# Half of each output projection multiplied between the heads of the attention, and added to x there

## Chip, cores and metric

One core of one Trainium2 chip runs the whole program. The metric is device microseconds (us) of one execution. Three timed executions of the kernel before took 4341.31 us in the median (4336.28 to 4342.41).

## The reference, cut to what matters

Two layers over 640 tokens (one tile of 128 context tokens, four tiles of 128 latent tokens), model width 1024. Each layer mixes tokens, adds the result to x, and then runs an expert network (PEER), which takes most of the time and is not touched here.

```
even layer:  oa = gated linear attention(h) -> rms_norm * silu      # (tokens, 512)
             ob = latent attention(h), 8 heads of 64                # (tokens, 512)
             x  = x + gate * (concat[oa, ob] @ w_out)               # w_out (1024, 1024)
odd layer:   oc = pool_mixer(h)                                     # (tokens, 512)
             od = windowed attention(h), 8 heads of 64              # (tokens, 512)
             x  = x + gate * (concat[oc, od] @ w_out)
```

The product with w_out is a sum over 1024 rows: 512 belong to oa (or oc), which is finished before the attention starts, and 512 to ob (or od).

## The kernel before, in words

Each engine has its own program (`block.tensor`, `block.vector`, `block.scalar`, `block.gpsimd`, `block.sync`), written out in order by hand; semaphores join them. Everything is float32.

**Streams of PSUM.** TensorE (PE) opens banks in order from three streams of two banks each: `open_d` (emptied by VectorE, DVE), `open_a` (emptied by ScalarE, ACT) and `open_s` (attention scores). `open_d` waits until all banks of its stream but the last one opened have been emptied (`d_free`). `copied()` waits until both streams are empty.

**The mixed vector.** `hT` holds eight slices of 128 rows: slices 0 to 3 are oa (or oc), written before the attention starts; slices 4 to 7 are the attention's output, written by `turn_out` (L645) once per tile.

**Attention.** `mla()` (even) and the second half of `odd()` loop over five query tiles `qt`. Tile 0 sees one key tile; tiles 1 to 4 of the even layer see five, of the odd layer three, four, four and three. `heads()` runs eight heads as a pipeline. Per turn of the loop PE does `scores(h + 2)` (L518), `turn(h + 1)`, the transposes of the softened scores (L532, L535), `product(h)` (L544), and then whatever `between(h)` holds. DVE does the maximum of the scores `biggest(h + 2)` (L1563; in the odd layer L1665, L1670), a reciprocal, the copy of the transposes `turned(h + 1)` (L1580), the scaling of the product (L1594), and then `between(h)`. ACT does the exponentials (L942, L973), in the even layer also the copy of the fifth transposed block (L846), and one square root per tile behind head 3, which needs a table load.

**Between the heads.** In both layers DVE prepares the next tile's queries there, in parts 0 to 5: part 3 (squares and their sum) behind head 3, part 4 behind head 4, part 5 (rotary embedding, L1479 to L1482) behind head 5. PE has queries work in the even layer alone, behind heads 0 to 2 (L599, L607). Tile 4 has no next tile and so nothing between its heads.

**Output projection.** `out_project` runs after the attention: two column halves `n` by five token tiles `t`, which is ten pieces. PE multiplies eight slices (L708); DVE multiplies the result by the gate (L1687) and adds it to x (L1689). Weights come through a ring of two slots, each 2 MB transfer issued by SyncE once the slot's last reader is done; `slot_done()` notes who that was. When the last sum is done, `x_done` lets the next norm start.

Of the kernel before, what the change touches and what calls it, by code (L numbers as in the profile page):

```python
# [26 lines left out]
ALU = mybir.AluOpType  # L27
# [52 lines left out]
def build_program(nc, a):  # L80

    ctx = ExitStack()
    with ctx:
# [208 lines left out]
        mod_rows = nc.dram_tensor("mod_rows", (2, 6 * D), F32, kind="Internal").ap()  # L292
        routing = nc.dram_tensor("routing", (NR, P, NB, RGROUP, TB), F32, kind="Internal").ap()

        def window_tiles(qt):

            return [0] if qt == 0 else [t for t in (qt - 1, qt, qt + 1) if 1 <= t < NT] + [5]
# [5 lines left out]
        def _(pe):  # L303
# [9 lines left out]
                pe.wait_ge(sem[f"slot_in{n % 2}"], 16 * (n // 2 + 1))  # L313
                return ring[:, n % 2, :]

            def slot_done():

                freed[item[0] - 1] = (last_stream[0], me.n[last_stream[0]])

            def mark(name):  # L320
                marks[name] = dict(me.n)
# [4 lines left out]
                pe.wait_ge(sem["a_free"], me.n["a_full"])  # L326

            last_stream = ["d_full"]

            def open_d():  # L330

# [189 lines left out]
            def heads(scores, probs_of, pT_of, tiles, v_of, between=None):  # L521
# [28 lines left out]
                for h in range(NH):  # L550
# [5 lines left out]
                    if between:  # L556
                        between(h)

            def mla():
                w = slot()  # L560
                w_uq = w[:, 0:2048].rearrange("p (k n) -> p k n", k=2)
                w_uk = w[:, 2048:3072].rearrange("p (k n) -> p k n", k=2)
                w_uv = w[:, 3072:4096].rearrange("p (k n) -> p k n", k=2)
                def keys_and_values(kt):
                    pe.wait_ge(*(me.due("ckv_ready") if kt < NT else (sem["ctx_in"], 32)))
                    ckv = pe_[:, kt, CKV0:CKV0 + 256] if kt < NT else ctx_ckv
                    out = open_d()
                    for k in range(2):
                        last = tr(out[:, P * k:P * (k + 1)], ckv[:, P * k:P * (k + 1)], ident)
                    last.then_inc(sem["d_full"], 1)  # L570
                    pe.wait_ge(sem["d_free"], me.n["d_full"])
                    for wk, opened, full in ((w_uk, open_d, "d_full"), (w_uv, open_a, "a_full")):
                        out = opened()
                        for k in range(2):
                            last = mm(out[:, :], ckvT[:, P * k:P * (k + 1)], wk[:, k, :], start=(k == 0), stop=(k == 1))
                        last.then_inc(sem[full], 1)

                keys_and_values(0)
                for kt in range(6):
                    if kt + 1 < 6:  # L580
                        keys_and_values(kt + 1)
                    pe.wait_ge(*me.due("k_ready"))
                    for g in range(2):
                        out = open_a()
                        for i in range(4):
                            h = 4 * g + i
                            last = tr(out[:, P * i:P * (i + 1)], qk[:, P * h:P * (h + 1)], ident)
                        last.then_inc(sem["a_full"], 1)
                    mark(("keys", kt))
                copied()  # L590
                turned_at = {}

                def queries(qt, part):

                    if part == 0:
                        pe.wait_ge(*me.due("ckv_ready"))
                        out = open_d()
                        for k in range(2):
                            last = tr(out[:, P * k:P * (k + 1)], pe_[:, qt, CQ0 + P * k:CQ0 + P * (k + 1)], ident)  # L599
                        last.then_inc(sem["d_full"], 1)  # L600
                        turned_at[qt] = me.n["d_full"]
                    elif part < 3:
                        at = 512 * (part - 1)
                        pe.wait_ge(sem["d_free"], turned_at[qt])
                        out = open_d()
                        for k in range(2):
                            last = mm(out[:, :], ckvT[:, P * k:P * (k + 1)], w_uq[:, k, at:at + 512],  # L607
                                      start=(k == 0), stop=(k == 1))
                        last.then_inc(sem["d_full"], 1)
                        if qt == NT - 1 and part == 2:  # L610
                            slot_done()

                for part in range(3):
                    queries(0, part)
                for qt in range(NT):
                    pe.wait_ge(*me.due("q_ready"))
                    for g in range(2):
                        out = open_a()
                        for i in range(4):
                            h = 4 * g + i  # L620
                            last = tr(out[:, P * i:P * (i + 1)], qk[:, P * h:P * (h + 1)], ident)
                        last.then_inc(sem["a_full"], 1)
                    copied()
                    tiles = [0] if qt == 0 else [1, 2, 3, 4, 5]
                    mark(("scores", qt))

                    def scores(h):
                        q_lhs = qT[:, P * h:P * (h + 1)]
                        if qt == 0:
                            attend(q_lhs, [(kT[:, h, 0:P], 0, P)])  # L630
                        else:
                            attend(q_lhs, [(kT[:, h, P:P + 512], 0, 512), (kT[:, h, P + 512:P + 640], 512, P)])

                    heads(scores, lambda h: probs[:, h % 2, :], lambda h: pT[:, h % 2, :], tiles,
                          lambda kt, h: vals[:, kt, 64 * h:64 * h + 64],
                          (lambda h: queries(qt + 1, h)) if qt + 1 < NT else None)
                    turn_out()

            def turn_out():
# [8 lines left out]
            def odd():  # L648
# [29 lines left out]
                for qt in range(NT):  # L678
# [8 lines left out]
                    def scores(h):  # L687
# [4 lines left out]
                        if qt:  # L692
# [2 lines left out]

                    heads(scores, lambda h: probs2[:, h % 2, :], lambda h: pT2[:, h % 2, :], tiles,
                          lambda kt, h: (po_[:, kt, VD0 + 64 * (h // 4):VD0 + 64 * (h // 4) + 64] if kt < NT
                                         else vctx[:, 64 * (h // 4):64 * (h // 4) + 64]))
                    turn_out()

            def out_project():
                copied()
                for n in range(2):
                    w = slot().rearrange("p (k n) -> p k n", k=KD)
                    for t in range(NT):
                        out = open_d()
                        for k in range(KD):
                            last = mm(out[:, :], hT[:, k, P * t:P * (t + 1)], w[:, k, :], start=(k == 0), stop=(k == KD - 1))  # L708
                        last.then_inc(sem["d_full"], 1)
                    slot_done()  # L710

            def route(l):
                copied()
# [575 lines left out]
        def _(dve):  # L1289
# [5 lines left out]
            def take_d():  # L1295
                n = me.next("d_full")
                dve.wait_ge(sem["d_full"], n)
                return bank[(n - 1) % 2]
# [200 lines left out]
            def mla():  # L1499
# [35 lines left out]
                def queries(qt, part):  # L1535
# [15 lines left out]
                    elif part == 5:  # L1551
                        if qt:
                            rope_into(qk3[:, :, 64:128], qk3[:, :, 64:128], qt, NH)
                        signal("q_ready")

                for part in range(6):
                    queries(0, part)
                for qt in range(NT):
                    n = P if qt == 0 else 5 * P

                    def biggest(h):
                        out = take_s().rearrange("p a b -> p (a b)")
                        link(V.tensor_reduce(stat[:, 32 + h:33 + h], out[:, 0:n], AX.X, ALU.max))  # L1563
                        give(ts(stat[:, 32 + h:33 + h], stat[:, 32 + h:33 + h], -MLA_SCALE, None, ALU.mult), "m_ready")

                    heads(biggest, lambda h: pT[:, h % 2, 0:min(n, 512)], att_o,
                          (lambda h: queries(qt + 1, h)) if qt + 1 < NT else None)

            def heads(biggest, pT_of, dst, between):

# [39 lines left out]
            def odd():  # L1610
# [36 lines left out]
                        signal("q_ready")  # L1647

                me.after("a_full", marks[("odd_k", 5)]["a_full"])
                for part in range(6):  # L1650
                    queries(0, part)
                for qt in range(NT):
# [8 lines left out]
                    def biggest(h):  # L1661
                        out = take_s().rearrange("p a b -> p (a b)")
                        s_ = soft_s[:, h % 2, :]
                        for i, (at, w, m_at) in enumerate(parts):
# [6 lines left out]
                        give(ts(stat[:, 32 + h:33 + h], stat[:, 32 + h:33 + h], sink[:, h:h + 1], -1.0,  # L1671
                                ALU.max, ALU.mult), "m_ready")

                    heads(biggest, lambda h: pT2[:, h % 2, 0:n], att_o2,
                          (lambda h: queries(qt + 1, h)) if qt + 1 < NT else None)

            def out_project(l):

                me.after("out_cache", 32 * (l + 1))
                if l:  # L1680
                    dve.wait_ge(sem["gates_in"], 16 * 4)
                for n in range(2):
                    for t in range(NT):
                        out = take_d()
                        g = gate[:, 0, int(t > 0), 512 * n:512 * n + 512]
                        tmp = arena[:, 8192:8704]
                        give(tt(tmp, out[:, :], g, ALU.mult), "d_free")  # L1687
                        xs = x[:, t, 512 * n:512 * n + 512]
                        ins = tt(xs, xs, tmp, ALU.add)  # L1689
                        if n == 0 or t < NT - 1:  # L1690
                            link(ins)
                give(ins, "x_done")
# [359 lines left out]
```

## Time and profile before

| what | us |
|---|---|
| median of three timed executions | 4341.31 |
| the profiled execution | 4340.67 |
| its span in the trace | 4338.9 |
| even layer, latent attention of tiles 1 to 4 | 565.5 to 725.4 |
| even layer, output projection | 725.4 to 795.9 |
| odd layer, windowed attention of tiles 1 to 4 | 2557.7 to 2715.4 |
| odd layer, output projection | 2715.4 to 2788.9 |

Times inside the trace are microseconds from the span's start. Busy shares say which engine is occupied in a stretch; the granted clock (PEclk) is the share of full speed at which TensorE was allowed to run, 1.00 for 2.4 GHz and 0.50 for 1.2 GHz. In a timeline the bracket behind a row is the engine's idle time before it and what ended that.

### The profile page before, as it was taken

To read this page: it belongs to the slowest core of one execution; us is meant where nothing else is said; L and a number is where in the kernel's file an instruction comes from. 1 tells how busy PE (TensorE), PEld (TensorE's weight loads), DVE (VectorE), ACT (ScalarE), POOL (GpSimd) and SP (SyncE) were. 2 spreads that over 40 slices of the span, in tenths; PEclk is the share of its full clock that TensorE was granted. 3 is DMA by queue.
4 is the path that set the end of the run, shared out by engine and by line. 5 is a ranking of instruction groups with operands and counts; after the bars stand their busy time and mean duration, and the time that the engine had idled before them with its cause. 6 is when DMAs were issued, how large, how long until landed. Compare 5 with 4: busy or idle time off the path is not lost. (4 is left out here: it accounts for less than half of the span.)

```text
span 4338.9 us, 51269 instructions
## 1 busy us (share of the span) xinstructions
PE 3786.7 (87%) x17467; PEld 2941.2 (68%) x17467; DVE 3316.4 (76%) x6040; ACT 1257.2 (29%) x1998; POOL 1940.3 (45%) x1290
## 2 busy tenths in 40 slices
PE   7986578899569999999997958886569999999997
PEld 1445255434458999999996547454458999999997
DVE  0116464487978999999998166299988999999998
ACT  1121122100553333333332132100563333333332
POOL 0000000001686777778775000000586777777775
PEclk9987689899789999999998955898799999999999
DMA  6210000242369999999998100111269999999997
GB/s 254 80 60 5 2 1 20 107 152 97 95 186 351 406 401 406 406 403 402 406 403 312 71 22 1 49 39 39 82 190 348 404 404 404 403 406 402 405 405 310
DMA packets 319360, 1013.07 MB, mean 233 GB/s; under 512 B 24062, under 2 KB 122366, under 8 KB 296728
## 3 DMA queue, kind: packets, MB, share of 16 engines
q0 software_dynamic: 152512, 571.76, 33.7%
q1 hardware_dynamic: 166744, 440.06, 26.9%
q8 instruction: 49, 0.80, 0.1%
q14 instruction: 55, 0.45, 0.0%
HBM read 958.16 MB, written 53.56 MB: 233 GB/s over the span
## 5 line engine op out<-in xcount | busy, mean ns | idle before, releaser
L1240 POOL DMA_INDIRECT arena<-in_peer_v,picked x512 | 831.9, 1625 | 226.7 <-issue 123.5
L1240 POOL DMA_INDIRECT arena<-in_peer_u_rows,picked x512 | 777.7, 1519 | 321.5 <-DVE dots L1817 194.1
L770 PE MATMUL pair<-h_hi,u_hi 128*128 128x384 f32 x2048 | 689.4, 337 | 30.9 <-issue 30.9
L770 PE MATMUL pair<-h_hi,u_lo 128*128 128x384 f32 x2048 | 688.8, 336 | 0.0
L770 PE MATMUL pair<-h_lo,u_hi 128*128 128x384 f32 x2048 | 688.0, 336 | 0.0
L1837 DVE SCALAR_TENSOR_TENSOR gate<-arena,act,gate 128x1024 f32<-128x1024 f32 x512 | 640.8, 1279 | 6.7 <-DVE act L1829 5.3
L1817 DVE CUSTOM_DVE_ANT_0 arena<-arena 128x1024 f32<-128x1024 f32 x512 | 612.4, 1219 | 17.1 <-DVE dots L1823 16.5
L1199 POOL TENSOR_TENSOR arena<-arena 128x256 f32<-128x256 f32 x192 | 287.3, 1530 | 348.9 <-DVE arena L1785 348.7
L770 PEld LDWEIGHTS pair<-h_hi,u_hi 128*128 128x128 f32 x2048 | 387.1, 189 | 39.2 <-issue 34.4
L770 PEld LDWEIGHTS pair<-h_lo,u_hi 128*128 128x128 f32 x2048 | 387.1, 189 | 4.8
L1029 ACT ACTIVATE u_hi<-ring 128x2048 fp32r<-128x2048 f32 x128 | 245.5, 1920 | 491.5 <-DMA ring<-in_peer_u 491.5
L770 PEld LDWEIGHTS pair<-h_hi,u_lo 128*128 128x128 f32 x2048 | 386.6, 189 | 0.0
L1049 ACT ACTIVATE act_raw<-pair 128x384 f32<-128x384 f32 x256 | 126.1, 492 | 809.6 <-PE pair L770 794.9
L1792 DVE TENSOR_TENSOR u_lo<-ring,u_hi 128x2048 fp32r<-128x2048 f32 x128 | 294.4, 2300 | 51.0 <-ACT u_hi L1029 46.2
L782 PE MATMUL bank<-v_hi,act_hi 128*128 128x512 f32 x1024 | 317.5, 391 | 0.0
L782 PE MATMUL bank<-v_hi,act_lo 128*128 128x512 f32 x1024 | 316.8, 391 | 0.0
L782 PE MATMUL bank<-v_lo,act_hi 128*128 128x512 f32 x1024 | 316.6, 390 | 0.0
L758 PE MATMUL pair<-arena 128*128 128x128 f32 x1536 | 223.9, 298 | 90.3 <-ACT arena L1012 49.7
L1785 DVE TENSOR_TENSOR arena<-arena,const 128x1024 f32<-128x1024 f32 x192 | 285.6, 1548 | 13.0 <-PE pair L758 9.8
L721 PE MATMUL bank<-hT,ring 128*128 128x128 f32 (+1 forms) x1024 | 292.8, 445 | 3.1 <-DVE hT L1362 3.1
L1796 DVE TENSOR_TENSOR v_lo<-ring,v_hi 128x2048 fp32r<-128x2048 f32 x128 | 292.6, 2286 | 0.0
L1279 POOL DMA_DIRECT2D arena<-in_subkeys x2 | 1.1, 542 | 641.7 <-DVE x L1689 641.7
(302 smaller groups left out, 5925.1 us busy)
## 6 DMA issues: line engine op xcount, KB each, us to landing
ring<-in_peer_u SPq DMA_DIRECT2D x128, 1024.0 KB
ring<-in_peer_v SPq DMA_DIRECT2D x128, 1024.0 KB
routing<-arena SPq DMA_DIRECT2D x24, 2048.0 KB, 8.7
arena<-routing SPq DMA_DIRECT2D x64, 768.0 KB
ring<-in_w_ada SPq DMA_DIRECT2D x12, 2048.0 KB, 7.7
ring<-in_w_ada POOLq DMA_DIRECT2D x12, 2048.0 KB, 8.0
ring<-in_peer_wq SPq DMA_DIRECT2D x8, 2048.0 KB, 7.8
ring<-in_w_in SPq DMA_DIRECT2D x6, 2048.0 KB, 7.8
```

The lines of the kernel that those rows point to most:

```text
L721: last = mm(out[:, 0:n], w[:, k, P * (g % 4):P * (g % 4 + 1)], hT[:, k, at:at + n], start=(k == 0), stop=(k == KD - 1))
L758: last = mm(pair[:, n % 4, P * q:P * (q + 1)], hots[:, n % 4, 1, q, :], hots[:, n % 4, 0, q, :], start=True, stop=True)
L770: last = mm(pair[:, j, 0:TD], R(u[b][:, P * (KD * j + k):P * (KD * j + k + 1)]), R(h[:, k, :]), start=(k == 0 and i == 0), stop=(k == KD - ...
L782: last = mm(outs_at[2 * t + half], R(w[b][:, j, P * t:P * (t + 1)]), R(v[b][:, D * j + 512 * half:D * j + 512 * half + 512]), start=False, ...
L1029: do(R(u_hi[b][:, :]), u_raw[b], ACT.Copy).then_inc(sem["u_led"], 1)
L1199: nc.gpsimd.tensor_tensor(rows, rows, bc(cols[:, b, 2, 4 * n + 2:4 * n + 4], P, 2), ALU.mult).then_inc(sem["gated_p"], 1)
L1240: pool.indirect_dma_start(gathered[:, b, :], None, rows, bass.IndirectOffsetOnAxis(picked[:, n:n + 1], 0)).then_inc(sem[f"row_in{b}"], 16)
L1785: tt(hots[:, m % 4], bc(cols[:, b, 0:2, 4 * n:4 * n + 4], P, 3), bc(bc(iota, 4, 1), 2, 1), ALU.is_equal).then_inc(sem["hot_ready"], 1)
L1792: tt(R(u_lo[b][:, :]), u_raw[b], u_hi[b][:, :], ALU.subtract).then_inc(sem["u_split"], 1)
L1796: tt(R(v_lo[b][:, :]), v_raw[b], v_hi[b][:, :], ALU.subtract).then_inc(sem["v_split"], 1)
L1817: V.tensor_tensor_reduce(gathered[:, b, :], gathered[:, b, :], h_nat[:, s_, :], 1.0, 0.0, ALU.mult, ALU.add, dots16[:, q:q + 1]).then_inc( ...
L1837: stt(acc[:, s_, :], gathered[:, b, :], act16[:, q:q + 1], acc[:, s_, :], ALU.mult, ALU.add).then_inc(sem["row_used"], 1)
```

## The change

Ten pieces per layer of the product with slices 0 to 3 are computed inside the attention's loop: `early_out((qt, h))`, called last in `between`. A table gives for each (qt, h) the piece (n, t). In the even layer the pieces stand behind heads (1, 3), (1, 6), (2, 3), (2, 6), (3, 3), (3, 7), (4, 1), (4, 3), (4, 5), (4, 7); in the odd layer behind heads 1, 4 and 7 of tiles 1, 2 and 3 and behind (4, 1). PE opens a bank of the d stream and multiplies four slices; DVE multiplies by the gate and adds to x, as before. `out_project` keeps ten pieces, but with slices 4 to 7 alone, and does the gate and the sum again for each. Both w_out weights now stay in the ring from the first early piece to the end.

```diff
+        early = [{(1, 3): (0, 0), (1, 6): (0, 1), (2, 3): (0, 2), (2, 6): (0, 3), (3, 3): (0, 4),
+                  (3, 7): (1, 0), (4, 1): (1, 1), (4, 3): (1, 2), (4, 5): (1, 3), (4, 7): (1, 4)},
+                 {(1 + i // 3, (1, 4, 7)[i % 3]): (i // NT, i % NT) for i in range(2 * NT)}]
...
 PE:
+            def early_out(at):
+                piece = early[layer[0]].get(at)
+                if piece is None:
+                    return
+                n, t = piece
+                if t == 0:
+                    w_out.append(slot().rearrange("p (k n) -> p k n", k=KD))
+                    out_items.append(item[0] - 1)
+                out = open_d()
+                for k in range(4):
+                    last = mm(out[:, :], hT[:, k, P * t:P * (t + 1)], w_out[-1][:, k, :], start=(k == 0), stop=(k == 3))
+                last.then_inc(sem["d_full"], 1)
...
 PE, out_project:
-                        for k in range(KD):
-                            last = mm(out[:, :], hT[:, k, P * t:P * (t + 1)], w[:, k, :], start=(k == 0), stop=(k == KD - 1))
+                        for k in range(4, KD):
+                            last = mm(out[:, :], hT[:, k, P * t:P * (t + 1)], w_out[n][:, k, :], start=(k == 4), stop=(k == KD - 1))
...
 DVE:
+            def add_out(n, t, tmp):
+                out = take_d()
+                link(tt(tmp, out[:, :], gate[:, 0, int(t > 0), 512 * n:512 * n + 512], ALU.mult))
+                signal("d_free")
+                xs = x[:, t, 512 * n:512 * n + 512]
+                return tt(xs, xs, tmp, ALU.add)
+            def early_out(at):
+                piece = early[layer[0]].get(at)
+                if piece:
+                    if layer[0] and piece == (0, 0):
+                        dve.wait_ge(sem["gates_in"], 16 * 4)
+                    link(add_out(*piece, pe_[:, 2, 0:512] if layer[0] == 0 else po_[:, 1, 0:512]))
```

## Rows read from the trace of the kernel before

**Rows 1.** The page: the span in 40 slices, granted clock in tenths.

```profile
PEclk9987689899789999999998955898799999999999
```

**Rows 2.** Windows: from:to, length; busy us (instructions) of PE, PEld, DVE, ACT, POOL; granted clock, DMA, GB/s.

```profile
653.40:697.70 44.30, 33.31 (x175) 25.30 (x175) 26.27 (x53) 13.87 (x30) 0.00 (x0) 0.88 0.13 48
697.70:725.40 27.70, 25.15 (x156) 19.71 (x156) 16.94 (x40) 9.90 (x25) 0.00 (x0) 0.94 0.01 2
725.40:795.90 70.50, 68.90 (x160) 30.32 (x160) 13.84 (x20) 0.00 (x0) 0.00 (x0) 1.00 0.10 33
2557.70:2595.20 37.50, 29.69 (x113) 24.90 (x112) 25.71 (x67) 12.38 (x30) 0.00 (x0) 0.50 0.00 1
2639.20:2683.00 43.80, 38.11 (x138) 30.46 (x140) 28.93 (x67) 12.84 (x29) 0.00 (x0) 0.50 0.00 1
2683.00:2715.40 32.40, 28.04 (x108) 23.51 (x107) 21.19 (x64) 8.62 (x25) 0.00 (x0) 0.50 0.00 1
2715.40:2721.60 6.20, 6.18 (x8) 2.59 (x9) 0.00 (x0) 0.00 (x0) 0.00 (x0) 0.50 0.01 3
2721.60:2788.90 67.30, 65.80 (x154) 28.85 (x152) 13.82 (x20) 0.00 (x0) 0.00 (x0) 1.00 0.10 35
```

**Rows 3.** Groups by line, even output projection: xcount, busy us, mean ns, idle before.

```profile
L708 PE MATMUL bank<-ring,hT 128*128 128x512 f32 x160 | 68.9, 593 | 0.8 <-issue 0.8
L1687 DVE TENSOR_TENSOR arena<-bank,gate 128x512 f32<-128x512 f32 x10 | 6.9, 692 | 57.8 <-PE bank L708 57.8
L1689 DVE TENSOR_TENSOR x<-x,arena 128x512 f32<-128x512 f32 x10 | 6.9, 692 | 0.3
```

**Rows 4.** Timeline (start, us, engine, line), even tile 3 around head 3.

```profile
672.28 0.33 SPq L1117 DMA_DIRECT2D ring<-in_w_out  x1
...
675.88 1.23 DVE L1544 TENSOR_TENSOR arena<-arena 128x1024 f32<-128x1024 f32 x1
...
676.41 0.27 PE L535 MATMUL bank<-const,ring 128*128 128x128 f32 x1
...
678.64 1.28 ACT L855 ACT_TABLE_LOAD   x1 [3.21 <-DVE stat L1316]
...
680.18 0.28 ACT L846 ACTIVATE arena<-bank 128x128 f32<-128x128 f32 x1
...
680.55 2.36 PE L544 MATMUL bank<-arena 128*128 128x64 f32 x10 [3.87 <-issue]
```

**Rows 5.** The page's DMA issues: the ring's 2 MB transfer, us from issue to landing.

```profile
ring<-in_w_in SPq DMA_DIRECT2D x6, 2048.0 KB, 7.8
```

**Rows 6.** Timeline, end of even tile 3 and start of tile 4.

```profile
692.22 1.30 PE L544 MATMUL bank<-arena 128*128 128x64 f32 x10 [2.08 <-DVE arena L1580]
...
693.97 1.05 PE L645 MATMUL bank<-const,arena 128*128 128x128 f32 x4 [0.45 <-DVE arena L1594]
694.82 2.07 PE L621 MATMUL bank<-const,arena 128*128 128x128 f32 x8
```

**Rows 7.** Windows of the even attention, columns as in rows 2.

```profile
649.60:653.30 3.70, 2.97 (x12) 2.27 (x12) 0.01 (x1) 1.77 (x3) 0.00 (x0) 0.54 0.00 0
653.30:656.70 3.40, 2.40 (x8) 1.28 (x8) 1.75 (x3) 0.77 (x3) 0.00 (x0) 1.00 0.00 0
...
680.40:687.20 6.80, 6.65 (x26) 5.64 (x26) 4.25 (x8) 2.50 (x5) 0.00 (x0) 0.50 0.00 0
```

**Rows 8.** Timeline, the scores of two successive heads, even tile 4.

```profile
705.74 1.35 PE L518 MATMUL pair<-ring,arena 128*128 128x512 f32 x4
...
708.54 1.35 PE L518 MATMUL pair<-ring,arena 128*128 128x512 f32 x4
```

**Rows 9.** Timeline, two successive heads of odd tile 3.

```profile
2654.30 2.07 PE L518 MATMUL pair<-arena 64*128 64x384 f32 x4
...
2656.49 0.69 DVE L1665 SCALAR_TENSOR_TENSOR arena<-pair,const 128x512 f32<-128x512 f32 x1 [1.55 <-PE pair L518]
...
2658.95 2.07 PE L518 MATMUL pair<-arena 64*128 64x384 f32 x4
```

More of the change, by code:

```diff
@@ L314, in slot, with slot_done @@
                 return ring[:, n % 2, :]
-            def slot_done():
-                freed[item[0] - 1] = (last_stream[0], me.n[last_stream[0]])
+            def slot_done(n=None):
+                freed[item[0] - 1 if n is None else n] = (last_stream[0], me.n[last_stream[0]])
             def mark(name):
@@ L328, in _ @@
             last_stream = ["d_full"]
+            w_out, out_items = [], []
             def open_d():
@@ L557, in heads @@
                         between(h)
+            def early_out(at):
[10 more added lines that the diff above has]
+                last.then_inc(sem["d_full"], 1)
             def mla():
                 w = slot()
+                w_item = item[0] - 1
                 w_uq = w[:, 0:2048].rearrange("p (k n) -> p k n", k=2)
@@ L610, in queries @@
                         if qt == NT - 1 and part == 2:
-                            slot_done()
+                            slot_done(w_item)
                 for part in range(3):
@@ L632, in scores, with between @@
                             attend(q_lhs, [(kT[:, h, P:P + 512], 0, 512), (kT[:, h, P + 512:P + 640], 512, P)])
+                    def between(h):
+                        if qt + 1 < NT:
+                            queries(qt + 1, h)
+                        early_out((qt, h))
                     heads(scores, lambda h: probs[:, h % 2, :], lambda h: pT[:, h % 2, :], tiles,
-                          lambda kt, h: vals[:, kt, 64 * h:64 * h + 64],
-                          (lambda h: queries(qt + 1, h)) if qt + 1 < NT else None)
+                          lambda kt, h: vals[:, kt, 64 * h:64 * h + 64], between)
                     turn_out()
@@ L697, in odd @@
                           lambda kt, h: (po_[:, kt, VD0 + 64 * (h // 4):VD0 + 64 * (h // 4) + 64] if kt < NT
-                                         else vctx[:, 64 * (h // 4):64 * (h // 4) + 64]))
+                                         else vctx[:, 64 * (h // 4):64 * (h // 4) + 64]),
+                          lambda h: early_out((qt, h)))
                     turn_out()
@@ L703, in out_project @@
                 for n in range(2):
-                    w = slot().rearrange("p (k n) -> p k n", k=KD)
                     for t in range(NT):
                         out = open_d()
-                        for k in range(KD):
-                            last = mm(out[:, :], hT[:, k, P * t:P * (t + 1)], w[:, k, :], start=(k == 0), stop=(k == KD - 1))
+                        for k in range(4, KD):
+                            last = mm(out[:, :], hT[:, k, P * t:P * (t + 1)], w_out[n][:, k, :], start=(k == 4), stop=(k == KD - 1))
                         last.then_inc(sem["d_full"], 1)
-                    slot_done()
+                    slot_done(out_items[n])
+                w_out.clear()
+                out_items.clear()
             def route(l):
@@ L1554, in queries, with between @@
                         signal("q_ready")
+                def between(qt, h):
+                    if qt + 1 < NT:
+                        queries(qt + 1, h)
+                    early_out((qt, h))
                 for part in range(6):
@@ L1566, in mla @@
                     heads(biggest, lambda h: pT[:, h % 2, 0:min(n, 512)], att_o,
-                          (lambda h: queries(qt + 1, h)) if qt + 1 < NT else None)
+                          lambda h: between(qt, h))
             def heads(biggest, pT_of, dst, between):
@@ L1649, in odd, with between @@
                 me.after("a_full", marks[("odd_k", 5)]["a_full"])
+                def between(qt, h):
+                    if qt + 1 < NT:
+                        queries(qt + 1, h)
+                    early_out((qt, h))
                 for part in range(6):
@@ L1672, in biggest @@
                                 ALU.max, ALU.mult), "m_ready")
-                    heads(biggest, lambda h: pT2[:, h % 2, 0:n], att_o2,
-                          (lambda h: queries(qt + 1, h)) if qt + 1 < NT else None)
+                    heads(biggest, lambda h: pT2[:, h % 2, 0:n], att_o2, lambda h: between(qt, h))
+            def add_out(n, t, tmp):
[10 more added lines that the diff above has]
+                    link(add_out(*piece, pe_[:, 2, 0:512] if layer[0] == 0 else po_[:, 1, 0:512]))
             def out_project(l):
                 me.after("out_cache", 32 * (l + 1))
-                if l:
-                    dve.wait_ge(sem["gates_in"], 16 * 4)
                 for n in range(2):
                     for t in range(NT):
[L1684 to L1689, printed above, removed]
+                        ins = add_out(n, t, arena[:, 8192:8704])
                         if n == 0 or t < NT - 1:
```

## The prediction, made before the change was run

> **What bounds the kernel now.** I read the clock line of the page first, then windows by stage, then the timeline inside one tile of each layer. The expert stages fill most of the span at full clock and are not touched; the change concerns two stretches of about 230 us each. In the clock line [rows 1] the attention stages show as the dips to 8 (even) and to 5 (odd), so every matmul moved into them has to be priced at the clock granted there.
>
> The windows [rows 2] show three situations. In both output projections PE is busy 66 to 69 of 67 to 70 us at clock 1.00 and DVE 14: PE alone sets their end, and each of the ten pieces takes 68.9 / 10 = 6.89 us for eight slices, so 3.44 us for four [rows 3]. DVE needs 0.69 + 0.69 = 1.38 us per piece, hidden under the next piece. In the even attention PE is busy 33.3 of 44.3 us in tile 3 (tiles 1 and 2 look alike) at a mean clock of 0.88: it waits for other engines. In tile 4, which prepares no next queries, it is busy 25.2 of 27.7. In the odd attention the clock is 0.50 from end to end, PE is busy 38.1 of 43.8 us in tile 3 and DVE 28.9.
>
> The profiled execution took 4340.67 us, of which 1.8 lie outside its span; it is 0.6 below the median of the timed runs, so its sums carry over.
>
> **Even layer.** Removed: half of every piece of the projection, 10 x 3.44 = -34.4 us. DVE's 1.38 us per piece is still shorter than the 3.44 us that are left, so PE still sets the end.
>
> Pieces (1,3), (2,3), (3,3). After head 3's transposes PE stands idle for 3.87 us [rows 4]: the copy of the fifth transposed block is behind ACT's square root and its table load, and that waits for DVE's queries part 3. In the new order PE has the piece exactly there: the bank it needs is free before part 3 begins, so 3.44 us fit into 3.87. DVE takes up the piece after part 3 and spends 1.38 us before its next maximum; but the exponential that follows waits for the second table load anyway, so that delay mostly disappears. PE now has no gap, while before it ran the next 6.8 us at half clock [rows 7]. I take -0.5 each, -1.5 together (bounds: +1.4, DVE's part uncovered, and -2, if the clock gives back more).
>
> Pieces (1,6), (2,6), (3,7). At the tile's tail PE waits for DVE, which is in the rotary embedding, and the last product comes 2.08 us late [rows 6]. A piece behind head 6 needs a bank that only DVE's copy of head 7 frees, the same copy that the product waits for. So it starts no earlier than that product did and pushes it by 3.44. Behind head 7 it adds 3.44 plus 0.69 for the multiply, because `turn_out` waits until both streams are empty. But PE stays busy where it had idled, and the next transposes, 2.07 us for eight [rows 6], and the next tile's first scores would run at full clock: about 1.7 us back. So +2 each, +6 (bounds +1 to +5 each).
>
> Pieces (4,1), (4,3), (4,5), (4,7). A head of tile 4 takes 708.54 - 705.74 = 2.80 us [rows 8] with PE working back to back, nothing to hide in: 3 x 3.44 = 10.3, and 3.44 + 0.69 = 4.1 for (4,7), in front of the last `turn_out`. +14.4 (bounds 13 and 17). DVE idles while PE does the piece and then owes 1.38 us, PE's next scores take 1.35 of it [rows 8], and the exponential is not due for three steps.
>
> The second w_out block is issued at 672.28 [rows 4] and such a block lands after 7.8 us [rows 5], ahead of piece (3,7) near 693. It is released by the last queries matmul as before. The peer_wq blocks wait, as before, for the two halves of the projection; one comes 17 us before the end, enough for 7.8. SP and POOL issue the same transfers in the same order. Sum of the even layer: -34.4 - 1.5 + 6 + 14.4 = -15.5 us.
>
> **Odd layer.** Removed: -34.4 again. The first 6.2 us of this projection ran at 0.50 [rows 2]; it will still start from low clock, so this part is neither gained nor lost.
>
> Added: ten pieces. At half clock a piece is 6.9 us, at full clock 3.44. Nothing in the trace of before runs such matmuls between odd heads, so the bounds are 69 and 34 us for ten. What the clock does in front of a rise: in the projection it rose 6.2 us after dense matmuls began [rows 2], in the even layer after a stretch of 2.97 us busy [rows 7]. Heads of the odd layer keep PE busy before a piece already, which is why I take a value near the shorter: 3.3 us at low clock, which does half of that, 1.65 us' worth, and the remaining 1.8 at full clock. That is 5.1 us per piece.
>
> Given back: after the rise PE runs the following heads fast for a while. A head of tile 3 takes 4.65 us, in which DVE waits 1.55 for the scores [rows 9]; that wait goes, in the heads with no queries part. Behind head 7 the next tile's start gains, 2.1 us of scores per head at half clock [rows 9]. I count 1.7 us back per piece; DVE's 1.38 us of a piece is inside the first fast scores or costs up to 0.8, counted in this. So 5.1 - 1.7 = 3.4 per piece, +34 for ten. Each second piece stands behind head 4, where DVE has part 4 of the queries to do meanwhile; the bank rule makes PE wait there for the copy of head 5, which cancels that. Sum of the odd layer: -34.4 + 34 = about 0.
>
> The transfer of the gates for this layer is long over when the first piece asks for it, since it is issued when x of layer 0 is done, near 2376, 180 us earlier.
>
> Total: -15.5 + 0, so 4340.7 - 15.5 = 4325 for the profiled execution and 4326 against the median.
>
> On the clock the Trainium skill ("TensorE: Matmul & The Clock Gate", Part 4: PE-mode transpose) says that the full clock does not engage for transposes because they don't count as PE-busy in the same way. This trace disagrees: between 649.6 and 653.3 PE ran nothing but twelve transposes, and the clock then rose from about half to 1.00 [rows 7]. If the rule held it would be the fourth rival below.
>
> **Rivals.**
> 1. The odd heads stay at full clock once a piece has raised it. Then DVE bounds a tile: 28.9 us of work, 3 x 1.38, about 7 of start and tail, 40 instead of 43.8 for tiles 2 and 3; likewise 37 for 37.5 and 29 for 32.4 [rows 2], together 12 us less than before with the pieces inside. With -34.4 and 3 more from the projection's start: -49, in all -65, 4277. For it: the even heads mostly keep full clock. Against it: PE was busy 38 of 43.8 us at half clock and the clock never rose [rows 2]; at full clock the same work would leave PE idle for about half of the time.
> 2. The clock does not rise between odd heads, or falls at once: a piece costs 6.9 us behind PE that is already busy without a pause. +69 - 34.4 = +34 there, in all +19, 4360. It decides from 5 us net per odd piece, (34.4 + 15.5) / 10. Against it: the projection does start a rise within less than one old piece.
> 3. Pure displacement: the work is moved and nothing is hidden. Even pieces cost 3.44 each plus the multiplies, odd pieces 3.4 to 4: +-8, 4339. For it: eight of ten odd slots and four even ones lie where PE never waits.
> 4. Transposes keep no clock. Then nothing is given back after a piece: even tails cost 3 x 1.7 more, odd pieces 5.1 each. +5 and +17: +7, 4348. Against it the row just named. This is what the page of the Trainium skill cited above would make of it.
>
> **How the numbers follow.** My forecast 0.50 (its own range 4313 to 4335), rival 1 0.12 (also in part, 4280 to 4313), rival 2 0.12, rival 3 0.21, rival 4 0.05. A measurement of this kernel can tell about 0.2%, 8.7 us, from no change. Below 4332.6 lie most of the forecast (0.43) and all of rival 1: 0.55. Within 0.2% the rest of the forecast, rival 3 and half of rival 4: 0.32. Above 4350: rival 2 and some of rival 4: 0.13. The range for 8 in 10, 4300 to 4347, leaves out most of rival 1 and rival 2.
>
> **What would show it.** Right: each projection takes 36 to 38 us instead of 70 and 73; even tiles 1 to 3 grow by about 2 us each and show no PE gap of 3.9 us behind head 3; even tile 4 grows by 14; the odd attention grows by some 34 us with a mean clock between 0.55 and 0.75. Wrong: a DVE or ACT wait that grows in even tiles 1 to 3 by more than 3 us, an odd clock still at 0.50 (rival 2) or above 0.85 (rival 1), or a wait of PE on the ring's slot before (1,3) or (3,7).

## The result, and the profile after

The changed kernel takes 4354.62 us in the median (4348.78 to 4357.68, six executions) beside 4341.86 of the kernel before: ratio 1.0023, 95% interval 1.0013 to 1.0034. It is slower by some 13 us, where I had forecast 15 faster, and it lies outside my range. The profiled execution, 4348.78 us with a span of 4347.0, was the fastest of the six; its span is 8.1 longer than that of before, where the medians differ by 12.8. Of the 4.7 that are missing, 3.0 lie ahead of the first moved piece: the work there is the same in both kernels, but this trace reaches the first output transpose at 556.1 us and that of before at 559.1. The stretches that the change touches grew by 12.5 us together, as the table below shows, which fits the medians.

The clock line of the page after, beside [rows 1]: the two slices of the odd attention stand at 6 instead of 5.

```profile
PEclk9987689999889999999998966798789999999999
```

Windows by stage, columns as in [rows 2]: even tile 3, even tile 4, even projection; odd tile 3, odd tile 4, odd projection.

```profile
660.90:710.90 50.00, 39.91 (x190) 27.54 (x191) 29.03 (x57) 13.86 (x30) 0.00 (x0) 0.90 0.12 43
710.90:757.60 46.70, 40.29 (x189) 26.28 (x190) 22.49 (x48) 9.89 (x25) 0.00 (x0) 0.96 0.00 1
757.60:794.10 36.50, 34.30 (x80) 14.83 (x78) 13.85 (x20) 0.46 (x1) 0.26 (x1) 1.00 0.20 68
2664.70:2722.80 58.10, 47.14 (x162) 30.46 (x162) 33.06 (x73) 12.84 (x29) 0.00 (x0) 0.68 0.00 1
2722.80:2759.30 36.50, 30.62 (x116) 22.94 (x116) 22.56 (x66) 8.26 (x25) 0.00 (x0) 0.63 0.00 1
2759.30:2797.60 38.30, 36.18 (x80) 15.77 (x80) 13.84 (x20) 0.35 (x1) 0.00 (x0) 0.95 0.18 61
```

Measured from one tile's first output transpose (L645 before, L669 after) to the next, with the projection reaching to the next norm's first transpose, in both traces (these bounds differ by some us from those of the windows above):

```
us                 tile 1   tile 2   tile 3   tile 4   projection   sum of changes
even  before         46.2     44.3     44.3     30.0         80.8
even  after          52.9     48.9     50.0     47.8         46.6
      change         +6.7     +4.6     +5.7    +17.8        -34.2            +0.6
      forecast             +4.5 in all         +14.4        -34.4           -15.5
odd   before         37.0     43.7     43.4     33.7         84.4
odd   after          53.3     56.9     58.0     37.2         48.7
      change        +16.3    +13.2    +14.6     +3.5        -35.7           +11.9
      forecast                 +34 in all                   -34.4               0
```

The groups of the even projection, as in [rows 3]: half the matmuls, the same 593 ns each, and DVE still waits 21.5 us for PE.

```profile
L732 PE MATMUL bank<-ring,hT 128*128 128x512 f32 x80 | 34.6, 593 | 0.8 <-issue 0.8
...
L1720 DVE TENSOR_TENSOR x<-x,arena 128x512 f32<-128x512 f32 x10 | 6.9, 693 | 1.6 <-DVE arena L1717 1.6
L1717 DVE TENSOR_TENSOR arena<-bank,gate 128x512 f32<-128x512 f32 x10 | 6.9, 692 | 21.5 <-PE bank L732 21.5
```

So the saving came as forecast, and it was spent in the attention: 34.8 us in the even layer where I had 18.9, and 47.6 in the odd where I had 34. Where, the timelines show. Even tile 3 behind head 3, beside [rows 4]: the piece (L575, four matmuls that the trace lists as eight) stands where PE had idled 3.87 us, and DVE, coming from queries part 3, waits only 0.82 for it. From head 3's product to head 4's the tile takes 7.1 us, before 6.9, so this piece is hidden.

```profile
683.01 3.70 PE L575 MATMUL bank<-ring,hT 128*128 128x512 f32 x8 [0.64 <-DVE arena L1612]
683.31 1.23 DVE L1570 TENSOR_TENSOR arena<-arena 128x1024 f32<-128x1024 f32 x1
...
686.55 1.24 PE L523 MATMUL pair<-ring,arena 128*128 128x512 f32 x4
686.82 0.69 DVE L1717 TENSOR_TENSOR arena<-bank,gate 128x512 f32<-128x512 f32 x1 [0.82 <-PE bank L575]
```

Its tail, beside [rows 6]: the piece behind head 7 takes 4.91 us, part of it at half clock, DVE stands idle for 4.42 us meanwhile and `turn_out` (L669) comes 5.5 us behind DVE's scaling of head 7.

```profile
702.23 4.91 PE L575 MATMUL bank<-ring,hT 128*128 128x512 f32 x8
702.54 0.28 DVE L1626 TENSOR_SCALAR arena<-bank,stat 128x64 f32<-128x64 f32 x1 [2.11 <-PE bank L549]
707.24 0.69 DVE L1717 TENSOR_TENSOR arena<-bank,gate 128x512 f32<-128x512 f32 x1 [4.42 <-PE bank L575]
708.05 0.66 PE L669 MATMUL bank<-const,arena 128*128 128x128 f32 x4 [0.91 <-DVEq L1333]
```

Odd tile 3, piece (3,1), beside [rows 9]: 6.38 us, mostly at half clock; DVE idle for 6.03 of them; then DVE multiplies and adds, and only then takes the maximum (L1703). PE, now fast, soon waits for DVE (L537).

```profile
2679.05 6.38 PE L575 MATMUL bank<-ring,hT 128*128 128x512 f32 x8
2685.54 0.69 DVE L1717 TENSOR_TENSOR arena<-bank,gate 128x512 f32<-128x512 f32 x1 [6.03 <-PE bank L575]
2686.39 0.69 DVE L1720 TENSOR_TENSOR x<-x,arena 128x512 f32<-128x512 f32 x1 [0.16 <-DVE arena L1717]
2687.11 0.69 DVE L1703 SCALAR_TENSOR_TENSOR arena<-pair,const 128x512 f32<-128x512 f32 x1
2689.84 0.63 PE L537 MATMUL bank<-const,arena 128*128 128x128 f32 x4 [0.86 <-DVE arena L1612]
```

The granted clock of that piece and of the stretch behind it:

```profile
2679.00:2685.40 6.40, 6.35 (x9) 2.49 (x9) 0.44 (x2) 0.29 (x1) 0.00 (x0) 0.57 0.00 0
2685.40:2691.50 6.10, 5.24 (x34) 4.18 (x33) 5.46 (x12) 1.11 (x3) 0.00 (x0) 0.98 0.00 0
```

### The profile page after: what moved, and what is told of

It reads as the page before. It is cut to its first block and busy times, and to the rows that moved or that the text cites. A ratio compares the mean times of both kernels' runs of the same rounds, so it can differ in the third digit from the quotient of the medians.

```text
span 4347.0 us, 51368 instructions
## 1 busy us (share of the span) xinstructions
PE 3771.9 (87%) x17467; PEld 2914.5 (67%) x17467; DVE 3345.2 (77%) x6080; ACT 1256.4 (29%) x1998; POOL 1929.6 (44%) x1290
## 5 line engine op out<-in xcount | busy, mean ns | idle before, releaser
L1266 POOL DMA_INDIRECT arena<-in_peer_u_rows,picked x512 | 768.7, 1501 | 331.2 <-DVE dots L1863 203.8
```

What stands on the lines that cost most here:

```text
L1266: pool.indirect_dma_start(gathered[:, b, :], None, rows, bass.IndirectOffsetOnAxis(picked[:, n:n + 1], 0)).then_inc(sem[f"row_in{b}"], 16)
```

## The experiments

Ratios are to the kernel before, timed on the same chip beside each group of experiments: its median was 4343.81 us beside e1 to e4, 4346.57 beside w1, w2, k1 and k2, and 4343.90 beside l1, l2, e5 and b1. In brackets the 95% interval. e3 and e5 leave a part of x out, so they measure time alone.

**Each layer alone.** The table `early` emptied for the other layer.

```diff
e1:  early = [{... even as in the change ...}, {}]
e2:  early = [{}, {... odd as in the change ...}]
```

> The change in the even layer alone; the odd layer projects as before. My theory after reading the two traces: the even layer gains nothing net (attention 34.8 us longer, projection 34.2 shorter), the loss is all in the odd layer. So 4340 to 4344 us, ratio 0.999 to 1.001. Rival, that the profiled execution was a lucky one and the even layer costs several us too: 4347 or more.

> The change in the odd layer alone. Theory: every odd piece starts at half clock and takes 5.1 to 6.4 us, the odd attention grows by 47 us and the projection shrinks by 35.7: +12 us, 4353 to 4355. Rival, that part of the loss is in the even layer or an interaction of both: 4345 to 4349.

e1 took 4338.99 us, 0.9988 (0.9979 to 0.9997); e2 took 4356.57, 1.0029 (1.0016 to 1.0041). The loss is the odd layer's alone. The even layer by itself gains about 5 us in the median of its executions, a little below what I expected from one trace. Its tiles and projection in e1's trace add up to 246.3 us, beside 246.2 in the change and 245.6 before, so by the traces these 5 us don't lie in the stretches that the change touches, and where they come from is not shown.

**Pieces behind head 3 only.**

```diff
+ early = [{(1, 3): (0, 0), (2, 3): (0, 1), (3, 3): (0, 2)}, {}]
```

> Only pieces (1,3), (2,3), (3,3) of the even layer are early, all others are multiplied whole in the projection. Theory, a piece behind head 3 fills PE's 3.9 us gap and is free, even gives back up to 0.9 us: 10.3 to 13 us faster than before, 4328 to 4331. Rival, displacement, each of the three costs what it saves: 4340 to 4342. Second rival, half hidden: 4335.

4332.44 us, 0.9972 (0.9961 to 0.9983): 11.4 less for three pieces of 3.44. That is what full hiding would give, but the interval, 7 to 17 us less, holds the second rival's 4335 too, and the trace speaks for something between. The pieces are hidden where they stand: from head 3's product to head 4's takes 7.0 us instead of 6.9. But tiles 2 and 3 begin more slowly, the first product coming 11.4 us behind the output transposes instead of 9.5, and tiles 1 to 3 take 47.4, 47.3 and 47.3 us instead of 46.2, 44.3 and 44.3, at a mean clock of 0.82 where tiles 2 and 3 had 0.88. Tile 4 is 1.2 shorter and the projection 8.4, so the touched stretches gain only 2.4 us in this trace. Tile 3, beside [rows 2]:

```profile
657.25:704.59 47.34, 39.43 (x182) 28.15 (x182) 27.65 (x55) 13.86 (x30) 0.00 (x0) 0.82 0.12 45
```

**What of an odd piece is PE, what is DVE.** e3 cuts the columns that PE multiplies, e5 the arithmetic of DVE.

```diff
e3, PE:
-  mm(out[:, :], hT[:, k, P * t:P * (t + 1)], w[:, k, :], ...)
+  mm(out[:, 0:64], hT[:, k, P * t:P * (t + 1)], w[:, k, 0:64], ...)
e5, DVE:
-  link(add_out(*piece, ...))
+  take_d(); signal("d_free")
```

> The odd layer alone, and of each early piece PE multiplies only 64 of 512 columns (the rest of the product with slices 0 to 3 is left out); DVE's gate and sum stay whole. Theory, PE's time at half clock is the cost: a piece costs about 0.9 us of PE and nearly nothing net, the projection still shrinks by 35.7, so 4341 - 36 + 5 to 10 = 4310 to 4316. Rival, DVE's 1.4 us per piece and the handshakes are the cost (4.8 us per piece stays at 2 or more): 4325 or more.

> The odd layer alone as in e2, but DVE's multiply and sum are left out of the ten early pieces (their share of x is missing); it only frees the bank. Theory, DVE's 1.4 us are exposed behind a piece: 1.0 to 1.5 us each, 10 to 15 below e2's 4356, 4341 to 4346. Rival (my prediction's step, hidden under PE's next scores): 4353 or more.

e3: 4333.47 us, 0.9976 (0.9967 to 0.9985), 23 below e2 and not the 40 or more that I expected; the number lies where I had put the rival's. Its trace shows why: a thin piece still takes 1.97 us, of which its eight weight loads fill 1.78, the clock stays at 0.50 throughout, and the four tiles still grow by 6.1, 6.1, 6.1 and 2.5 us, which is 2.1 per piece. The cost of a thin piece is thus about its time on PE, and DVE's arithmetic fits into the time in which DVE waits for PE's slow scores (0.46 us of that wait are left ahead of the maximum, of 1.55 before). But the clock never rises here and a full piece does raise it, so e3 says little about a full piece; e5 takes DVE's part out of one.

```profile
2666.95 1.97 PE L578 MATMUL bank<-ring,hT 128*128 128x64 f32 x8
...
2669.03 0.69 DVE L1728 TENSOR_TENSOR arena<-bank,gate 128x512 f32<-128x512 f32 x1 [1.62 <-PE bank L578]
...
2671.03 0.69 DVE L1714 SCALAR_TENSOR_TENSOR arena<-pair,const 128x512 f32<-128x512 f32 x1 [0.46 <-PE pair L525]
```

e5: 4351.07 us, 1.0016 (1.0007 to 1.0025), 5.5 below e2: 0.55 per piece, half of what I expected and more than the nothing of the rival. The two intervals overlap, but the tiles agree: 199.3 us in e5's trace, 205.4 in e2's. In the same place of its trace the maximum starts at 2686.64 instead of 2687.11, since PE's scores aren't ready sooner.

```profile
2679.15 6.39 PE L578 MATMUL bank<-ring,hT 128*128 128x512 f32 x8
...
2686.64 0.69 DVE L1714 SCALAR_TENSOR_TENSOR arena<-pair,const 128x512 f32<-128x512 f32 x1 [7.03 <-PE pair L525]
```

**The clock by itself.** The extra matmuls multiply constants into a bank that nothing reads in the odd attention.

```diff
+ def spin(times):
+     for _ in range(times):
+         mm(pair[:, 1, :], ident, const[:, 0:512], start=True, stop=True)
  scores(0); scores(1)
+ spin(6 if tile 1 else 2)                       # odd tiles 1 to 4
  for h in range(NH):
+     spin(2 if h > 5 else 1)
```

> The kernel before, with 65 or so extra matmuls (128x512, result unused, into a PSUM bank that the odd attention leaves empty) between the odd heads of tiles 1 to 4, to keep PE busy. Theory: what bounds the odd heads is PE at half clock. With the extra work the clock stays at 1.00, DVE becomes the bound and the odd attention falls from 158 us to about 135: 4343 - 22 = 4321. Rival, the clock does not hold and the extra work is simply added (65 x 1.7 us at half clock): 4400 or more. Second rival, the clock holds but nothing is won because DVE bound the heads all along: 4343.

> The odd layer's early pieces as in the change, even layer as before, plus the same extra matmuls. Theory, an odd piece is dear only because it starts at half clock (5.1 to 6.4 us): at full clock it takes 3.5 to 3.7, and relative to the same kernel without early pieces it adds at most 20 us to the attention and takes 36 from the projection: 16 us faster than w1_spin, about 4305. Rival, the pieces' cost is the handshake and not the clock: as slow against w1_spin as the change was against before, +12.

That makes 52 extra matmuls of 512 columns, two entries each. w1: 4328.02 us, 0.9958 (0.9944 to 0.9972), 18.5 less, by doing more work. The four odd tiles take 144.0 us instead of 157.8 and the projection 3.4 less. Tile 3 takes 36.8 us instead of 43.4 at a clock of 1.00; tile 1, at whose start the clock was still at 0.50, takes 2.4 more.

```profile
2635.40:2672.20 36.80, 31.45 (x166) 20.02 (x162) 28.91 (x67) 12.84 (x29) 0.00 (x0) 1.00 0.00 1
```

w2: 4348.37 us, 1.0008 (0.9999 to 1.0017), and this overturned my theory. At a mean clock of 0.85 to 0.95 the odd tiles take 55.0, 54.3, 54.8 and 35.0 us, together 55 more than w1's: 5.5 per piece, more than the 4.8 of the change. Part of that is the extra matmuls' own doing: in w1 PE is already busy for 31.5 of tile 3's 36.8 us, so with three pieces of 3.7 the tile could not take less than 42.6. It takes 54.8. The trace shows two waits. PE waits ahead of the piece for DVE's copy, which the bank rule of `open_d` demands, and DVE then waits for nearly the whole piece. The clock falls again in the second wait and right behind the first, at 2695.2 and 2678.1 us. (The last line shows the first two of a piece's eight entries; that piece took 6.47 us.)

```profile
2677.59 5.40 PE L589 MATMUL bank<-ring,hT 128*128 128x512 f32 x8 [1.32 <-DVE arena L1635]
...
2683.10 0.69 DVE L1740 TENSOR_TENSOR arena<-bank,gate 128x512 f32<-128x512 f32 x1 [5.05 <-PE bank L589]
...
2696.37 2.08 PE L589 MATMUL bank<-ring,hT 128*128 128x512 f32 x2 [3.10 <-DVE arena L1635]
```

**The order by itself.** The piece moved behind the next scores on PE and behind the next maximum on DVE.

```diff
 PE:   if h + 2 < NH: scores(h + 2)
+      if h: early_out((tile, h - 1))
       if h + 1 < NH: turn(h + 1)
 DVE:  if h + 2 < NH: biggest(h + 2)
       reciprocal
+      if h: early_out((tile, h - 1))
       if h + 1 < NH: turned(h + 1)
```

> The change with one move: a piece of head h (all but head 7's) stands on PE behind scores(h + 3) instead of ahead of them, and on DVE behind biggest(h + 3). Theory after w2: DVE stands idle for the whole piece and PE's next scores feed a DVE that first owes 1.4 us, so PE's and DVE's times add up; with the scores first, DVE's maximum (1.0 us even, 1.6 odd) and the exponential run beside the piece. 15 pieces by 0.7 to 1.5 us: 10 to 20 us below the change's 4356, 4336 to 4346. Rival, the clock alone sets a piece's price: 4353 to 4358.

> w2 (odd pieces, extra matmuls) with the same move. There the clock is full most of the time, so the serial order is what is left: seven pieces of the odd layer by 1.2 to 1.6 us, 8 to 12 us below w2's 4348: 4336 to 4340. Rival, no effect of the order: 4346 to 4350.

The pieces behind head 7 keep their place, so 15 of the 20 move. l1: 4343.51 us, 0.9996 (0.9986 to 1.0005), some 12 below the change, as expected. Its trace puts 8.4 us of that into the odd tiles, 3.2 into even tile 4 and 0.7 into even tiles 1 to 3. l2: 4325.64, 0.9957 (0.9943 to 0.9970), 23 below w2 where I expected 8 to 12: with PE waiting less, the clock no longer dropped in tiles 2 and 3, so here order and clock act together. Tile 3 takes 46.6 us at 1.00 and a piece 3.70, of which DVE waits 1.77.

```profile
2665.89 3.70 PE L593 MATMUL bank<-ring,hT 128*128 128x512 f32 x8
2666.07 0.69 DVE L1740 SCALAR_TENSOR_TENSOR arena<-pair,const 128x512 f32<-128x512 f32 x1 [0.31 <-PE pair L525]
...
2669.70 0.69 DVE L1754 TENSOR_TENSOR arena<-bank,gate 128x512 f32<-128x512 f32 x1 [1.77 <-PE bank L593]
```

**Another place.** `in_keys` puts pieces among the key tiles, ahead of the attention, so that PE multiplies while DVE normalises keys.

```diff
k1:
+ for kt in range(6):                        # odd layer, PE
+     for piece in in_keys[1].get(kt, ()): half_piece(*piece)   # 1, 2, 2, 2, 2, 1 pieces
      pe.wait_ge(*me.due("k_ready"))
k2:  as k1, and
+ even early = {(1, 3): (0, 2), (2, 3): (0, 3), (3, 3): (0, 4)}, even in_keys = {2: [(0, 0)], 3: [(0, 1)]}
b1:  as k2, with spin as in w1
```

> The even layer as before; the odd layer's ten early pieces not between the heads but ahead of the attention, one or two behind each of the six key tiles, where PE is busy 2 of 10 us and comes from full clock. Theory: they find full clock and an idle PE; DVE pays 1.4 us each, or PE's 3.5 us of two pieces against DVE's 3.6 us per key tile bounds it: +15 to +22 us there, -36 in the projection, so -14 to -21: 4322 to 4329. Rival, the place doesn't matter (4.8 us per piece as between the heads): 4355.

> As k1, and in the even layer pieces (0,2), (0,3), (0,4) behind head 3 of tiles 1 to 3 and (0,0), (0,1) behind key tiles 2 and 3; the second column half is multiplied whole. Theory: the three behind head 3 save 10 as in e4, the two among the keys 3.4 - 1.4 each, and k1's gain comes on top: about 15 us below k1, 4308 to 4314. Rival, the key tiles of the even layer have no room: no better than e4 plus k1.

> The best so far, k2, plus w1's extra matmuls between the odd heads. Theory, the two gains are of different stretches and add: 4317.5 - 18.5 = 4299 (4295 to 4304). Rival, the odd attention now starts at another clock and keeps less of it: 4310.

k1: 4323.16 us, 0.9951 (0.9938 to 0.9965). k2: 4317.54, 0.9930 (0.9916 to 0.9943); beside k1 that is 6 less and not the 15 I expected. Its even tiles 1 to 3 show the cost that e4's show too: 47.3, 47.3 and 47.7 us instead of 46.2, 44.3 and 44.3. In k1 a piece costs DVE a short wait, since it has other work while PE multiplies, and the clock there is full: from the first to the last key transpose it is 1.00, where it was 0.50 before. From the end of the even projection to the first output transpose of the odd layer the trace takes 14.8 us more than before, 1.5 per piece, near DVE's 1.38. Here two pieces stand in a row on PE:

```profile
2515.06 7.03 PE L578 MATMUL bank<-ring,hT 128*128 128x512 f32 x16
...
2520.25 0.69 DVE L1736 TENSOR_TENSOR arena<-bank,gate 128x512 f32<-128x512 f32 x1
```

b1, the fastest kernel found: 4298.20 us, 0.9899 (0.9884 to 0.9914), 46 below the kernel before.

Means over the odd pieces of each trace, in us:

```
                 PE waits ahead   piece on PE   DVE idle for it
change                0.74            5.82           4.93
w2 (extra matmuls)    1.47            4.93           4.06
l2 (and the order)    0.25            3.69           1.70
k1 (among the keys)   0.10            3.61           0.57
```

## Why the prediction was wrong

**Confirmed.** The projections fell by 34.2 and 35.7 us (forecast 34.4 each), with PE still setting their end. In the change the pieces behind head 3 are hidden: between the products of heads 0 and 6 the three tiles grew by 1.9 us together, where I had -1.5 and named +1.4 each as the worst. Neither weights nor gates were waited for. The odd clock rose to a mean of 0.66 to 0.70 by tile, inside the 0.55 to 0.75 that I named.

**The step that failed: DVE's standing still during a piece was put at nothing.** I priced the pieces by PE's time and took DVE's 1.38 us behind each as hidden under PE's next scores, in both layers. The sum was short by 13.6 us in the odd attention and by 15.9 in the even one.

In the odd layer +34 for ten pieces measured 47.6, 4.8 each where I had 3.4. Two terms of it were off. The piece took 5.8 us and not 5.1: I had put the rise of the clock 3.3 us after its start, and it came 2.9 to 5.4 us after, 4.3 in the mean. And I gave back 1.7 us because DVE's wait of 1.55 per head would go; 1.0 came back. The wait does go, but then DVE is the bound, and the piece itself makes DVE idle. I had written that DVE's 1.38 us cost at most 0.8 (e5: 0.55) and never priced DVE's standing still for 4.9 us per piece, because at half clock PE seemed the only bound. l1 shows that the order is a large part: with seven of the ten pieces one step later the odd tiles give back 8.4 of the 13.6 us, and the kernel as a whole is level with before. A fuller clock alone doesn't cure it: w2, at 0.85 to 0.95, still pays 5.5 us per piece, and the same work in l2's order takes 23 us less.

In the even layer tile 4, which I priced at PE's 3.44 per piece and one multiply, grew by 17.8 us instead of 14.4, although it began 2.1 us faster than before: a stage that looks PE-bound with DVE busy 16.9 of 27.7 us [rows 2] lets a new step pass at PE's price only if DVE has something to do meanwhile. l1, where it has, gives 3.2 us of that back. The tails were forecast at +2 each; tiles 1 to 3 grew by 17 instead of 4.5, and from head 6's product to the tile's end they took 6.1, 5.0 and 6.0 us longer than before. The piece there ran partly at half clock, 4.9 to 6.2 us, and DVE's 1.4 us stood in front of the last scaling or its 0.69 us of multiplying in front of `turn_out`. I had charged one multiply for head 7 alone, and counted on a clock kept full by the piece. It had fallen before the piece began: in tile 3 at 694.5 us, when PE was waiting 2.28 us for DVE's copy, while the piece started at 702.2. A sign of being wrong that I had named came here: in tile 3's tail DVE waits 2.11 and then 4.42 us for PE, where before it waited 1.04 once.

**Rivals.** Rival 1: w1 shows that the odd heads can run at full clock and then faster, but its 40 us for a tile with pieces inside were not reached even at 1.00 (l2, 46.6, with extra matmuls in it). Rival 2, the dear odd pieces, had the right sign and the nearest number (4360); but its reason, a clock that doesn't rise, is not what happened, and its even layer was the same wrong -15.5, so that the number came near is luck. Rival 3's own terms add up to 4342 or more, not to the 4339 that I wrote. The rival I lacked is the serial hand-off. Rival 4: the clock fell again 7 to 10 us after each rise in the odd attention, which that rule would also give, but a stretch of transposes alone was followed by its rise in [rows 7], and no run here separates transposes from matmuls in the odd heads.

**Open.** Executions of one kernel differ by 3 to 12 us. The traces put little of that into the attention: tiles whose code and surroundings are unchanged repeat within 0.4 us, while the stretch ahead of the attention, where all kernels but k2 and b1 are the same, ends anywhere from 556.1 to 564.7 us. So the even layer's net is +0.6 us by the stretches touched and -5 by e1's median (its interval: 1 to 9 less), and the runs don't settle it. The even tails' excess is described and not explained by a run of its own: l1, which moves the pieces behind head 6 and not the one behind head 7, leaves tiles 1 to 3 about as long. That e4's and k2's even tiles run longer at a lower clock is read from their traces; why they do was not tested.

## What to carry to other kernels

Work moved into another engine's idle time is cheap only where both of its ends are covered: the producer must not wait for its buffer, and the consumer must have other work until the result is there. Put such a step behind the producer's next piece of ordinary work, so that the consumer has that to do meanwhile (l1), or look for a stage in which the consumer is busy anyway (k1). And before matmuls are moved, read the granted clock of the place they go to; where PE runs at half clock and the next engine has slack, keeping PE busy can be worth more than the move.

## What the runs showed of the hardware

In w1 52 matmuls whose result nobody reads made the kernel 18.5 us faster (ratio 0.9958, 0.9944 to 0.9972): between odd heads PE was busy 38.1 of 43.8 us at 0.50 [rows 2] and the clock never rose by itself in tiles 1 to 4, and with the extra matmuls it held 1.00 in tiles 3 and 4. Matmuls of 64 columns took hardly longer than their weight loads: in e3 a piece's eight entries at half clock took 1.97 us, 1.78 of them with weight loads, where the eight of 512 columns took 6.38 in the change's piece (3,1), the end of it already at full clock.
